# A decoder layer on one core: x tiles fetched at once and the first two projection tiles done per token tile, and a second query tile inside the residual loop

## The chip, the cores and the metric

The kernel runs on one core of a Trainium2 chip. The metric is the device time of one execution in microseconds. The engines are named as the profile names them: PE is TensorE (PEld its weight loads, which run beside the products), DVE is VectorE, ACT is ScalarE, POOL is GpSimd, SP is SyncE, which here only issues transfers.

## The reference, cut to what matters

One decoder layer for 512 prompt tokens and 64 sample tokens (8 sequences of 8), model width 2048, in float32:

```
h  = rmsnorm(x, g_mix_pre);  z = h @ w_in          # 56 column tiles of 128
mix = retention (8 heads) and differential attention (4 heads) over z
x  = x + rmsnorm(mix @ w_out, g_mix_post)
h  = rmsnorm(x, g_mem_pre);  q = h @ w_mem_q       # 4 query tiles of 128
x  = x + rmsnorm(softmax(q mk^T / sqrt(128)) mv @ w_mem_o, g_mem_post)
x  = x + rmsnorm(relu(rmsnorm(x, g_mlp_pre) @ w_up)**2 @ w_down, g_mlp_post)
mem_k, mem_v = rmsnorm(mem, mem_norm_g) @ w_mem_k, ... @ w_mem_v
```

Outputs are the new x, the new retention states, the new keys and values, and the memory keys and values.

## The kernel before, in words

**Layout.** Activations lie transposed: width on the 128 partitions (16 chunks), the 576 tokens along the free side. Every large product is made from two-part operands: a value is split into a high part (rounded, type fp32r) and a low part (the rest), for weights as `w_hi` and `w_lo`, for activations as `act_hi` and `act_lo`. One output tile of 128 columns by 576 tokens is the sum over 16 chunks of hi x hi, hi x lo and lo x hi, in two halves of 288 tokens that lie in two PSUM banks: 96 products. Each product carries its own weight load. The helper `parts` (line 1842) issues the six products of one chunk, `tile` (line 1850) a whole tile.

**Weights.** Stripes of 2048 columns of weights come by SP into `w_raw`, of which there are two. ACT copies a stripe to `w_hi` (helper `hi`, line 807), DVE subtracts to get `w_lo` (helper `lo`, line 1162). There are two buffers of each, so a stripe is split when the tile that used its buffer is through; semaphores `s_tile` (tiles done on PE), `s_evac` (tiles taken out of PSUM), `s_whi` and `s_wlo` (splits done) order this. All orders are written out by hand, one program for each engine.

**The opening** (lines 485 to 495 on SP, 624 to 638 on POOL, 815 to 859 on ACT, 1167 to 1225 on DVE, 1860 to 1928 on PE). x comes in seven tiles of 128 tokens, in the order prompt 0 to 3, sample (64 tokens), then two of memory. POOL asks for them, into two buffers `xin`: tile p waits till PE has turned tile p - 2 and ACT has squared it. The norm weights (seven of 16 rows, one of 2, and four lambda vectors) are gathered as 118 rows in `g_rows`: ACT issues eight loads, POOL four and the page table. When all of them and the page table are there (`s_gain`, `s_lam`), PE turns the rows into `gT` (line 1888). For each x tile PE turns it in four quarters (`x_turn`), DVE multiplies a quarter with the norm weights out of PSUM (steps g0 to g3), ACT rounds it to `act_hi`, and DVE subtracts for `act_lo` (steps l0 to l3). That is `x_norm`, on DVE in the order g0 g1 l0 g2 l1 g3 l2 l3. ACT squares each x tile as well; when all five are squared, a root, a reciprocal and five products with diagonals (line 1907) give `rstd_b`, the scale of each token, on all partitions. It is multiplied in when a tile is taken out of PSUM.

The first two projection tiles use `half_tile`: tokens 0 to 287 of tiles 0 and 1 when three x tiles are done, tokens 288 to 575 after the fifth. Then come x tile 5 and projection tile 2, x tile 6 and tile 3 (`early_tile`), the memory keys and values, and the main stream. Tiles 0 to 3 are rotated when they are taken out (`z_turn`, line 1240).

**The residual loop ahead of the query tiles** (ACT 1001, DVE 1618, PE 2210 and 2250 to 2255). For each of 16 chunks DVE scales y and adds it to x, ACT makes the high part and the square of it, DVE the low part (line 1615). PE sums the squares over the partitions with two products of ones of type f32 (each recorded as two, line 2218) and does the six products of the first query tile for that chunk (`first_tile`). Then ACT and DVE make the root and its reciprocal (1018, 1628), and three more query tiles follow, each with its own weight split, taken out with the scale at line 1657. `residual` and `first_tile` serve a second time ahead of the MLP.

Of the kernel before, what the change touches and what calls it, by code (L numbers as in the profile page):

```python
# [14 lines left out]
F32 = mybir.dt.float32  # L15
F32R = mybir.dt.float32r
I32 = mybir.dt.int32
ALU = mybir.AluOpType
# [142 lines left out]
def program(nc, x_prompt, x_sample, mem_prompt, state_ret, cache_k, cache_v, cache_mk, cache_mv, pages,  # L161
# [5 lines left out]
    with ctx:  # L167
# [48 lines left out]
        st = ExitStack()  # L216
        mem_hi = sb("mem_hi", [P, KC, MEM], F32R, st)
        mem_lo = sb("mem_lo", [P, KC, MEM], F32R, st)
        xin = [sb(f"xin{b}", [P, D], F32, st) for b in range(2)]
# [110 lines left out]

        c_wpad = z_out[0][:, 0:MC * C_PAD + 32]
# [12 lines left out]
        s_lam = sem("s_lam")  # L344
        s_rcs = sem("s_rcs")
# [10 lines left out]
        s_xin = [sem(f"s_xin{b}") for b in range(2)]  # L356
# [15 lines left out]
        EARLY = 4  # L372

# [245 lines left out]
        def _(pool):  # L619
# [16 lines left out]
            pool.dma_start(dcs[:], dcs_d).then_inc(s_dcs, 16)  # L636
            for p in range(2, len(order)):
                x_load(p)
# [37 lines left out]

            page = [pool.value_load(pg[0:1, i:i + 1], min_val=0, max_val=NPOOL - 1) for i in range(DB * NPG)]
# [124 lines left out]
        def _(act):  # L802
# [12 lines left out]
            for g, row in ((g_mix_pre, G_MIX_PRE), (g_mix_post, G_MIX_POST), (g_mem_pre, G_MEM_PRE), (g_mem_post, G_MEM_POST),  # L815
                           (g_mlp_pre, G_MLP_PRE), (g_mlp_post, G_MLP_POST), (g_memn, G_MEMN)):
                act.dma_start(g_rows[row:row + KC, :], g.rearrange("a (c p) -> (a c) p", p=P)).then_inc(s_gain, 16)
            act.dma_start(g_rows[G_SUB:G_SUB + 2, :], subln.rearrange("a (c p) -> (a c) p", p=P)).then_inc(s_gain, 16)

            def x_norm(p):  # L820

                t = order[p]
                rows = x_tiles[t][1]
                act.wait_ge(s_xin[p % 2], 16 * (p // 2 + 1))
                act.wait_ge(e_act.sem, e_act.before("sq", p))
                e_act.did(nc.scalar.activation(sq_junk[0:rows, :], xin[p % 2][0:rows, :], ACT.Square,
                                               accum_out=ssq[0:rows, t:t + 1]), "sq")
# [25 lines left out]
            x_norm(5)  # L853
            hi(4, 0, 0, 3)
            x_norm(6)
            act.wait_ge(e_act.sem, e_act.of("sq", NT + 1))
# [144 lines left out]
            def residual(k, g_pre, stripe, tile):  # L1001

                hi(stripe + 1, 0, (stripe + 1) % 2, tile + EXTRA)
                roots(2 * k)
                with act.Fori(0, KC // 2) as i:
                    for b in range(2):
                        act.wait_ge(n_x, i * 2 + (k * KC + b + 1))
                        act.sem_inc(s_idle, 1)
                        x = xT[:, bass.ds(2 * i + b, 1), :].rearrange("p a t -> p (a t)")
                        nc.scalar.activation(act_hi[:, bass.ds(2 * i + b, 1), :].rearrange("p a t -> p (a t)"), x,  # L1010
                                             ACT.Copy, scale=gT[:, bass.ds(2 * i + (g_pre + b), 1)]).then_inc(n_hi, 1)

# [28 lines left out]
            for j in range(1, MH):  # L1041
                hi(S_MQ + j + 1, 0, (j + 1) % 2, G_MQ + EXTRA + j)
# [111 lines left out]
        def _(dve):  # L1154
# [15 lines left out]
            for k in range(2):  # L1170
                V.tensor_tensor(lamv[:, k:k + 1], gT[:, G_LAM + 2 * k:G_LAM + 2 * k + 1], gT[:, G_LAM + 2 * k + 1:G_LAM + 2 * k + 2],
                                ALU.mult).then_inc(m_dve, 1)

            V.tensor_scalar(gT[:, G_SUB:G_SUB + 2], gT[:, G_SUB:G_SUB + 2], 1.0 - LAM_INIT, None, ALU.mult).then_inc(m_dve, 1)

# [23 lines left out]
            x_norm(0)  # L1199
            dve.wait_ge(m_act, 1)  # L1200
# [5 lines left out]
            x_norm(1)  # L1206
            lo(0, 0)
            x_norm(2)
            lo(1, 1)
# [30 lines left out]
            def z_turn(n, b, stored):  # L1240
# [7 lines left out]
                for half in range(2):  # L1248
                    cols = slice(half * TH, (half + 1) * TH)
                    ins = V.tensor_tensor(z_out[b][:, cols], G[2 * b + half][:, 0:TH], rstd_b[:, cols], ALU.mult)  # L1250
# [400 lines left out]
            for j in range(MH):  # L1651
                if j:
                    lo(S_MQ + j + 1, (j + 1) % 2)
                dve.wait_ge(s_tile, G_MQ + EXTRA + j + 1)
                for half in range(2):
                    cols = slice(half * TH, (half + 1) * TH)
                    ins = V.tensor_tensor(c_q[:, j, cols], G[2 * (j % 2) + half][:, 0:TH], rstd_b[:, cols], ALU.mult)
                ins.then_inc(s_evac, 1)

# [176 lines left out]
        def _(pe):  # L1836
# [23 lines left out]
            def x_turn(p):  # L1860
                rows = x_tiles[order[p]][1]
                pe.wait_ge(s_xin[p % 2], 16 * (p // 2 + 1))
                for q in range(4):
                    if p >= 1:
                        pe.wait_ge(e_dve.sem, e_dve.of(f"g{q}", p - 1))
                    for j in range(4):
                        ins = nc.tensor.transpose(A[q][:, j * P:j * P + rows], xin[p % 2][0:rows, (4 * q + j) * P:(4 * q + j + 1) * P],
# [15 lines left out]

            pe.wait_ge(s_cst, 16)
            x_turn(0)
            pe.wait_ge(s_gain, 16 * 8)
            pe.wait_ge(s_lam, 16 * 5)
            nc.tensor.transpose(G[0][:, 0:G_ROWS], g_rows[:], ident[0:G_ROWS, 0:G_ROWS]).then_inc(m_pe, 1)
# [3 lines left out]
            for p in range(1, 4):  # L1892
                x_turn(p)
            pe.wait_ge(s_wlo, 1)
            pe.wait_ge(e_dve.sem, e_dve.of("l3", 2))
            pe.wait_ge(m_act, 1)
            half_tile(0, 0)
            x_turn(4)
            pe.wait_ge(s_wlo, 2)
            half_tile(1, 0)  # L1900
            for c in range(NT):
                rows = tok(c)[1]
                pe.wait_ge(m_dve, 7 + c)
                if c == 0:
                    pe.wait_ge(e_dve.sem, e_dve.of("l3", NT - 1))
# [317 lines left out]

            def out_tile(n):
# [26 lines left out]
            first_tile(0, S_MQ, G_MQ)  # L2251
            for j in range(1, MH):
# [213 lines left out]
```

## Time and profile before

| what | us |
|---|---|
| median of 3 runs (3130.74 to 3131.6) | 3131.55 |
| the profiled execution | 3132.76 |
| its span, first to last instruction | 3131.1 |
| PE busy in it | 3042.4 |
| DVE busy | 1301.3 |
| ACT busy | 768.9 |

The profile is of one execution. Engine shares are of the span; a row of a group names line, engine, operation and tiles with count, busy time and mean duration. Ends of matmuls are modelled and they overlap, so the time from the start of one to the start of the next says more of PE's pace than a duration does.

### The profile page before, as it was taken

To read this page: it belongs to the slowest core of one execution; us is meant where nothing else is said; L and a number is where in the kernel's file an instruction comes from. 1 tells how busy PE (TensorE), PEld (TensorE's weight loads), DVE (VectorE), ACT (ScalarE), POOL (GpSimd) and SP (SyncE) were. 2 spreads that over 40 slices of the span, in tenths; PEclk is the share of its full clock that TensorE was granted. 3 is DMA by queue.
4 is the path that set the end of the run, shared out by engine and by line. 5 is a ranking of instruction groups with operands and counts; after the bars stand their busy time and mean duration, and the time that the engine had idled before them with its cause. 6 is when DMAs were issued, how large, how long until landed. Compare 5 with 4: busy or idle time off the path is not lost.

```text
span 3131.1 us, 53528 instructions
## 1 busy us (share of the span) xinstructions
PE 3042.4 (97%) x22485; PEld 2931.0 (94%) x22485; DVE 1301.3 (42%) x1860; ACT 768.9 (25%) x836; POOL 165.1 (5%) x265
## 2 busy tenths in 40 slices
PE   7999999999999998998999999999999999999996
PEld 6899999989899997787999999999999999999995
DVE  6544245445554536467332322323323233232346
ACT  4311123223222233334212112122121121221221
POOL 0000012221211010000000000000000000000001
PEclk9999999999999999999999999999999999999997
DMA  5433535554656361513222223222222222222241
GB/s 181 156 103 107 151 117 162 167 168 149 218 162 222 134 211 54 148 55 115 81 80 81 91 73 89 82 80 80 80 80 86 77 87 86 80 80 80 80 141 61
DMA packets 398904, 355.04 MB, mean 113 GB/s; under 512 B 9554, under 2 KB 362052, under 8 KB 396772
## 3 DMA queue, kind: packets, MB, share of 16 engines
q1 hardware_dynamic: 377456, 269.18, 28.7%
q0 software_dynamic: 21136, 84.66, 7.9%
q8 instruction: 56, 0.92, 0.1%
q14 instruction: 28, 0.23, 0.0%
q10 hardware_dynamic: 228, 0.06, 0.0%
HBM read 305.62 MB, written 48.23 MB: 113 GB/s over the span
## 4 chain that ended last, share of the span: by engine, by line
PE 90%; issue 4%; DVE 3%; DMA 1%; POOL 1%; ACT 1%; DVEq 0%; POOLq 0%; ACTq 0%
PE gemm L1846 81%; PE aux L1949 2%; PE gemm L1926 1%; PE gemm L1875 1%; DVE yT L1606 1%; DVE yT L1827 1%; PE aux L1989 1%; PE aux L2005 1%; DMA d_vp<-in_cache_diff_v 0%; POOL d_kp L682 0%; POOL d_vp L682 0%; ACT w_hi L812 0%; DVE rstd_b L1596 0%; DMA pg<-in_page_table 0%; PE aux L2152 0%
## 5 line engine op out<-in xcount | busy, mean ns | idle before, releaser
L1846 PE MATMUL gemm<-act_hi,w_hi 128*128 128x288 f32 x4544 | 994.8, 300 | 7.8 <-DVE act_lo L1615 4.3
L1846 PE MATMUL gemm<-act_hi,w_lo 128*128 128x288 f32 x4544 | 973.4, 296 | 0.0
L1846 PE MATMUL gemm<-act_lo,w_hi 128*128 128x288 f32 x4544 | 972.7, 296 | 0.0
L1846 PEld LDWEIGHTS gemm<-act_hi,w_hi 128*128 128x128 f32 x4544 | 731.6, 189 | 41.2 <-issue 18.1
L1846 PEld LDWEIGHTS gemm<-act_lo,w_hi 128*128 128x128 f32 x4544 | 732.6, 189 | 0.0
L1846 PEld LDWEIGHTS gemm<-act_hi,w_lo 128*128 128x128 f32 x4544 | 732.6, 189 | 0.0
L1165 DVE TENSOR_TENSOR w_lo<-w_raw,w_hi 128x2048 fp32r<-128x2048 f32 x216 | 494.4, 2289 | 198.3 <-ACT w_hi L812 74.2
L1846 PE MATMUL gemm<-u_lo,w_hi 128*128 128x288 f32 x2048 | 438.6, 296 | 0.0
L1846 PE MATMUL gemm<-u_hi,w_hi 128*128 128x288 f32 x2048 | 438.5, 296 | 0.0
L1846 PE MATMUL gemm<-u_hi,w_lo 128*128 128x288 f32 x2048 | 438.4, 296 | 0.0
L1846 PEld LDWEIGHTS gemm<-u_hi,w_hi 128*128 128x128 f32 x2048 | 330.2, 189 | 0.0
L1846 PEld LDWEIGHTS gemm<-u_lo,w_hi 128*128 128x128 f32 x2048 | 330.2, 189 | 0.0
L1846 PEld LDWEIGHTS gemm<-u_hi,w_lo 128*128 128x128 f32 x2048 | 330.2, 189 | 0.0
L812 ACT ACTIVATE w_hi<-w_raw 128x2048 fp32r<-128x2048 f32 x90 | 172.1, 1912 | 335.8 <-PE gemm L1846 280.0
L1118 ACT ACTIVATE w_hi<-w_raw 128x2048 fp32r<-128x2048 f32 x63 | 120.8, 1918 | 516.6 <-PE gemm L1846 516.6
L1777 DVE TENSOR_TENSOR yT<-yT,gemm 128x288 f32 x192 | 78.5, 450 | 362.9 <-PE gemm L1846 362.9
L1755 DVE SCALAR_TENSOR_TENSOR z_out<-gemm,rstd_b 128x288 f32<-128x288 f32 x128 | 52.6, 452 | 405.1 <-PE gemm L1846 405.0
L1110 ACT ACTIVATE z_out<-z_out 128x576 f32<-128x576 f32 x64 | 43.9, 685 | 613.8 <-DVE z_out L1755 613.8
L1105 ACT ACTIVATE w_hi<-w_raw 128x2048 fp32r<-128x2048 f32 x63 | 120.1, 1906 | 77.4 <-PE gemm L1846 76.1
L794 POOL DMA_DIRECT2D act_hi<-x_scratch x1 | 0.6, 574 | 1818.6 <-PE gemm L1846 1818.6
L1760 DVE TENSOR_TENSOR u_lo<-z_out,u_hi 128x576 f32 (+1 forms) x64 | 48.5, 758 | 112.4 <-ACT u_hi L1112 112.4
L1235 DVE TENSOR_TENSOR z_out<-gemm,rstd_b 128x288 f32<-128x288 f32 x48 | 19.7, 451 | 99.1 <-PE gemm L1846 99.1
(309 smaller groups left out, 1922.9 us busy)
## 6 DMA issues: line engine op xcount, KB each, us to landing
w_raw<-in_w_mlp_up SPq DMA_DIRECT2D x64, 1024.0 KB, 6.4
w_raw<-in_w_mlp_down SPq DMA_DIRECT2D x64, 1024.0 KB, 5.3
w_raw<-in_w_in SPq DMA_DIRECT2D x56, 1024.0 KB, 5.7
w_raw<-in_w_out SPq DMA_DIRECT2D x16, 1024.0 KB, 6.0
z_scratch<-z_out SPq DMA_DIRECT2D x56, 288.0 KB, 2.1
r_zin<-z_scratch POOLq DMA_DIRECT2D x8, 1152.0 KB, 6.3
xin<-in_x_prompt POOLq DMA_DIRECT2D x8, 1024.0 KB, 6.8
d_z<-z_scratch POOLq DMA_DIRECT2D x12, 576.0 KB, 7.1
```

The source lines that it names most:

```text
L812: nc.scalar.activation(w_hi[b][:], w_raw[b][:], ACT.Copy).then_inc(s_whi, 1)
L1105: nc.scalar.activation(w_hi[(b + 1) % 2][:], w_raw[(b + 1) % 2][:], ACT.Copy).then_inc(s_whi, 1)
L1110: nc.scalar.activation(u_s[:], u_t[:], ACT.Square).then_inc(u_sq, 1)
L1118: nc.scalar.activation(w_hi[(b + 1) % 2][:], w_raw[(b + 1) % 2][:], ACT.Copy).then_inc(s_whi, 1)
L1165: V.tensor_tensor(w_lo[b][:], w_raw[b][:], w_hi[b][:].bitcast(F32), ALU.subtract).then_inc(s_wlo, 1)
L1606: V.tensor_tensor(y, y, n_rt[:], ALU.mult).then_inc(n_t, 1)
L1755: ins = V.scalar_tensor_tensor(out=u_t[:, cols], in0=G[2 * b + half][:, 0:TH], scalar=0.0, in1=rstd_b[:, cols], op0=ALU.max, op1=ALU.mult)
L1760: V.tensor_tensor(u_lo[:, k, :].rearrange("p a t -> p (a t)"), u_s[:], u_hi[:, k, :].rearrange("p a t -> p (a t)").bitcast(F32), ALU.subtr ...
L1777: ins = V.tensor_tensor(y, y, G[2 * m + half][:, 0:TH], ALU.add)
L1827: V.scalar_tensor_tensor(out=yT[:, c, :], in0=yT[:, c, :], scalar=gT[:, G_MLP_POST + c:G_MLP_POST + c + 1], in1=x_back[:, c, :], op0=ALU.m ...
L1846: ins = M(out[half][:, 0:TH], w[b][:, cols], x[:, k, half * TH:(half + 1) * TH], start=first and n == 0, stop=last and n == 2)
L1949: return nc.tensor.transpose(out, in_, ident[0:rows, 0:rows])
```

## The change

**Opening.** There are five `xin` buffers, three of them in the room of `mem_hi` and `mem_lo`; POOL asks for all five x tiles at once and for the page table after them, and waits for that only where it reads it. The lambda rows and three of the gains are issued by SP, which waits for them ahead of the first weight stripe; ACT issues five loads. PE turns the norm weights first. ACT runs a Square of one column early, splits w0 behind x tile 0 and w1 behind x tile 1, and squares each x tile behind its rounding. DVE puts the split of w0 ahead of the lambda steps. `half_tile` is replaced by `piece(n, p)`: projection tile n for x tile p, 48 products of 128 tokens (64 for the sample), the prompt in one bank and the sample in the next. At the evacuation of tiles 0 and 1 the columns are cut at 512 and not at 288.

**Residual loop.** In the first use `first_tiles` does the second query tile four chunks behind the first, in two more banks. The third weight stripe is split behind the loop, ahead of root and reciprocal; the third query tile goes to banks of its own (`q_bank`) without a wait for an evacuation. The second use, ahead of the MLP, stays.

```diff
+        x_early = [sb(f"x_early{b}", [P, D], F32, alias) for b in range(PC - 1)]
-        xin = [sb(f"xin{b}", [P, D], F32, st) for b in range(2)]
+        xin = [sb(f"xin{b}", [P, D], F32, st) for b in range(2)] + x_early
+        q_bank = [G[0:2], G[2:4], A[0:2], G[2:4]]
...
             sp.dma_start(cst[:], cst_d).then_inc(s_cst, 16)
+            for k, v in enumerate((lq1, lk1, lq2, lk2)):
+                sp.dma_start(g_rows[G_LAM + k:G_LAM + k + 1, :], v).then_inc(s_lam, 16)
+            for g, row in gains[4:]:
+                sp.dma_start(g_rows[row:row + KC, :], g.rearrange("a (c p) -> (a c) p", p=P)).then_inc(s_lam, 16)
+            sp.wait_ge(s_lam, 16 * (4 + len(gains[4:])))
...
             def x_load(p):
                 src, rows = x_tiles[order[p]]
-                if p >= 2:
-                    pool.wait_ge(e_pe, 4 * (p - 1))
-                    pool.wait_ge(e_act.sem, e_act.of("sq", p - 2))
-                pool.dma_start(xin[p % 2][0:rows, :], src).then_inc(s_xin[p % 2], 16)
-
-            x_load(0)
-            x_load(1)
-            for k, v in enumerate((lq1, lk1, lq2, lk2)):
-                pool.dma_start(g_rows[G_LAM + k:G_LAM + k + 1, :], v).then_inc(s_lam, 16)
-            pool.dma_start(pg[:], pages.rearrange("(a b) n -> a (b n)", a=1)).then_inc(s_lam, 16)
+                if p >= NT:
+                    pool.wait_ge(e_pe, 4 * (p - NT + 1))
+                    pool.wait_ge(e_act.sem, e_act.of("sq", p - NT))
+                pool.dma_start(xin[p % NT][0:rows, :], src).then_inc(s_xin[p % NT], 16)
+
+            for p in range(NT):
+                x_load(p)
+            pool.dma_start(pg[:], pages.rearrange("(a b) n -> a (b n)", a=1)).then_inc(s_pg, 16)
...
             act.wait_ge(s_setup, 3)
+            nc.scalar.activation(rms[:, 0:1], eps[:], ACT.Square)
             x_norm(0)
+            hi(0, 0, 0, None)
+            x_square(0)
             act.wait_ge(m_pe, 2)
             nc.scalar.activation(lamv[:, 2:4], G[1][:, 0:2], ACT.Exp).then_inc(m_act, 1)
             x_norm(1)
-            hi(0, 0, 0, None)
+            hi(1, 0, 1, None)
+            x_square(1)
             x_norm(2)
-            hi(1, 0, 1, None)
             x_norm(3)
+            x_square(2)
             x_norm(4)
+            x_square(3)
+            x_square(4)
...
+                if k == 0:
+                    hi(stripe + 2, 0, stripe % 2, tile + EXTRA + 1)
                 for half in range(2):
                     act.wait_ge(n_used, (k + 1) * KC + 2)
...
             x_norm(0)
+            lo(0, 0)
+            for k in range(2):
+                V.tensor_tensor(lamv[:, k:k + 1], ...
+            x_norm(1)
+            lo(1, 1)
             dve.wait_ge(m_act, 1)
...
-            x_norm(1)
-            lo(0, 0)
             x_norm(2)
-            lo(1, 1)
...
                 low(k, KC - 1, g_pre)
+                if k == 0:
+                    lo(stripe + 2, stripe % 2)
                 dve.wait_ge(n_rts, 4 * k + 4)
...
-            def half_tile(n, half):
-
+            def piece(n, p):
+
+                c0, rows = tok(p)
+                out = G[2 * n][:, c0:c0 + rows] if p < PC else G[2 * n + 1][:, 0:rows]
+                pe.wait_ge(s_wlo, n + 1)
+                pe.wait_ge(e_dve.sem, e_dve.of("l3", p))
                 for k in range(KC):
                     for i, (w, x) in enumerate(((w_hi, act_hi), (w_hi, act_lo), (w_lo, act_hi))):
-                        ins = M(G[2 * n + half][:, 0:TH], w[n][:, k * P:(k + 1) * P], x[:, k, half * TH:(half + 1) * TH],
+                        ins = M(out, w[n][:, k * P:(k + 1) * P], x[:, k, c0:c0 + rows],
                                 start=k == 0 and i == 0, stop=k == KC - 1 and i == 2)
                 return ins
...
             pe.wait_ge(s_cst, 16)
+            pe.wait_ge(s_gain, 16 * 5)
+            pe.wait_ge(s_lam, 16 * (4 + len(gains[4:])))
+            nc.tensor.transpose(G[0][:, 0:G_ROWS], g_rows[:], ident[0:G_ROWS, 0:G_ROWS]).then_inc(m_pe, 1)
             x_turn(0)
...
+            x_turn(1)
             pe.wait_ge(m_dve, 4)
             pe.wait_ge(s_setup, 3)
             M(G[1][:, 0:2], ones[:], lamv[:, 0:2], start=True, stop=True).then_inc(m_pe, 1)
...
+            piece(0, 0)
+            x_turn(2)
+            piece(0, 1)
+            piece(1, 0)
+            x_turn(3)
+            piece(1, 1)
+            piece(0, 2)
+            x_turn(4)
+            piece(1, 2)
+            piece(0, 3)
+            piece(1, 3)
             pe.wait_ge(m_act, 1)
-            half_tile(0, 0)
-            x_turn(4)
-            pe.wait_ge(s_wlo, 2)
-            half_tile(1, 0)
+            piece(0, 4).then_inc(s_tile, 1)
             for c in range(NT):
...
                 M(out, ones[0:rows, :], diag_t[c % 2][0:rows, 0:rows], start=True, stop=True).then_inc(m_pe, 1)
-            for n in range(2):
-                half_tile(n, 1).then_inc(s_tile, 1)
+            piece(1, 4).then_inc(s_tile, 1)
...
+            def first_tiles(stripe, tile, behind):
+                pe.wait_ge(s_wlo, stripe + 2)
+                pe.wait_ge(s_evac, tile)
+                def chunk(m, c):
+                    return parts((stripe + m) % 2, c, slice(c * P, (c + 1) * P), act_hi, act_lo, G[2 * m:2 * m + 2], c == 0, c == KC - 1)
+                for c in range(KC):
+                    pe.wait_ge(n_xsq, c + 1)
+                    for half in range(2):
+                        ins = M(A[2 + half][:, 0:TH], ones[:], n_sq[c % 2][:, half * TH:(half + 1) * TH], start=c == 0, stop=c == KC - 1)
+                    ins.then_inc(n_used, 1)
+                    if c >= behind:
+                        chunk(1, c - behind)
+                    pe.wait_ge(n_lo, c + 1)
+                    ins = chunk(0, c)
+                ins.then_inc(s_tile, 1)
+                for c in range(KC - behind, KC):
+                    ins = chunk(1, c)
+                ins.then_inc(s_tile, 1)
...
-            first_tile(0, S_MQ, G_MQ)
-            for j in range(1, MH):
+            first_tiles(S_MQ, G_MQ, 4)
+            for j in range(2, MH):
                 pe.wait_ge(s_wlo, S_MQ + j + 1)
-                pe.wait_ge(s_evac, G_MQ + j - 1)
-                tile(j % 2, P, 0, KC, act_hi, act_lo, j % 2).then_inc(s_tile, 1)
+                if j == 3:
+                    pe.wait_ge(s_evac, G_MQ + j - 1)
+                for k in range(KC):
+                    ins = parts(j % 2, k, slice(k * P, (k + 1) * P), act_hi, act_lo, q_bank[j], k == 0, k == KC - 1)
+                ins.then_inc(s_tile, 1)
```

## Rows read from the trace of the kernel before

**Rows 1.** The page, busy time of each engine and the costliest group.
```profile
PE 3042.4 (97%) x22485; PEld 2931.0 (94%) x22485; DVE 1301.3 (42%) x1860; ACT 768.9 (25%) x836; POOL 165.1 (5%) x265
...
L1846 PE MATMUL gemm<-act_hi,w_hi 128*128 128x288 f32 x4544 | 994.8, 300 | 7.8 <-DVE act_lo L1615 4.3
```
**Rows 2.** Chain of waits, 0 to 145 us: start us, us, what.
```profile
4.68 10.02 DMA pg<-in_page_table
...
36.84 7.96 PE gemm L1875 x48
...
52.46 0.23 PE aux L1907 x2
...
54.32 13.00 PE gemm L1875 x96
67.32 1.75 PE aux L1867 x16
69.06 12.78 PE gemm L1846 x96
```
**Rows 3.** Timeline, 0 to 70 us: start us, us, engine, line, tiles.
```profile
10.18 3.65 PE L1867 MATMUL aux<-cst,xin 128*128 128x128 f32 x16 [10.18 <-DMA xin<-in_x_prompt]
...
15.83 1.41 DVE L1189 TENSOR_TENSOR gx<-aux,gT 128x512 f32<-128x512 f32 x2
...
20.19 1.43 DVE L1196 TENSOR_TENSOR act_lo<-gx,act_hi 128x512 fp32r<-128x512 f32 x2
...
39.38 0.44 PE L1875 MATMUL gemm<-act_lo,w_hi 128*128 128x288 f32 x1
...
39.62 0.44 PE L1875 MATMUL gemm<-act_hi,w_lo 128*128 128x288 f32 x1
...
39.85 0.34 PE L1875 MATMUL gemm<-act_hi,w_hi 128*128 128x288 f32 x1
...
61.12 0.82 DVE L1250 TENSOR_TENSOR z_out<-gemm,rstd_b 128x288 f32<-128x288 f32 x2 [5.94 <-PE gemm L1875]
...
65.20 2.27 DVE L1165 TENSOR_TENSOR w_lo<-w_raw,w_hi 128x2048 fp32r<-128x2048 f32 x1
```
**Rows 4.** Busy time by stretch: PE, PEld, DVE, ACT, POOL, then granted clock, DMA.
```profile
36.80:39.80 3.00, 2.96 (x12) 2.99 (x13) 2.02 (x1) 2.84 (x3) 0.00 (x0) 1.00 0.88 186
```
**Rows 5.** Chain of waits, 1205 to 1310 us.
```profile
1250.06 0.76 DVE yT L1606
...
1252.43 0.76 DVE yT L1606
...
1261.85 39.20 PE gemm L1846 x294
```
**Rows 6.** Timeline of PE in the residual loop, with a backlog.
```profile
1233.79 1.13 PE L2218 MATMUL aux<-z_out,ones 128*128 128x288 f32 x4
...
1235.56 1.13 PE L2218 MATMUL aux<-z_out,ones 128*128 128x288 f32 x4
```
**Rows 7.** DMA issues of the first 100 us: size, median us to landing.
```profile
w_raw<-in_w_in SPq DMA_DIRECT2D x4, 1024.0 KB, 11.2
...
cst<-const_cst SPq DMA_DIRECT2D x1, 194.0 KB, 2.7
...
```
**Rows 8.** Timeline of PE and PEld: spacing of long and of short products.
```profile
107.99 0.39 PE L1926 MATMUL gemm<-w_hi,mem_hi 128*128 128x512 f32 x1
108.22 0.39 PE L1926 MATMUL gemm<-w_hi,mem_lo 128*128 128x512 f32 x1
...
813.88 0.99 PEld L2160 LDWEIGHTS aux<-r_v,r_kd 128*128 128x128 f32 x8
...
832.09 1.20 PEld L2194 LDWEIGHTS aux<-ones,r_sq 128*128 128x128 f32 x10
```
**Rows 9.** Groups of PEld by shape: 128 and 32 weight columns.
```profile
L1926 PEld LDWEIGHTS gemm<-w_lo,mem_hi 128*128 128x128 f32 x64 | 12.0, 188 | 2.5
...
L2340 PEld LDWEIGHTS aux<-c_vc,z_out 128*32 128x32 f32 x128 | 3.2, 109 | 3.0 <-issue 3.0
```

More of the change, by code:

```diff
@@ L344, in program @@
         s_lam = sem("s_lam")
+        s_pg = sem("s_pg")
         s_rcs = sem("s_rcs")
@@ L355, in program @@
         s_evac = sem("s_evac")
-        s_xin = [sem(f"s_xin{b}") for b in range(2)]
+        s_xin = [sem(f"s_xin{b}") for b in range(NT)]
         s_zst = [sem(f"s_zst{b}") for b in range(2)]
@@ L372, in program @@
         EARLY = 4
+        gains = ((g_mix_pre, G_MIX_PRE), (g_mix_post, G_MIX_POST), (g_mem_pre, G_MEM_PRE), (g_mem_post, G_MEM_POST),
+                 (g_mlp_pre, G_MLP_PRE), (g_mlp_post, G_MLP_POST), (g_memn, G_MEMN))
         block = ctx.enter_context(nc.Block())
@@ L625, in x_load @@
                 src, rows = x_tiles[order[p]]
-                if p >= 2:
-                    pool.wait_ge(e_pe, 4 * (p - 1))
-                    pool.wait_ge(e_act.sem, e_act.of("sq", p - 2))
-                pool.dma_start(xin[p % 2][0:rows, :], src).then_inc(s_xin[p % 2], 16)
-            x_load(0)
-            x_load(1)
-            for k, v in enumerate((lq1, lk1, lq2, lk2)):
-                pool.dma_start(g_rows[G_LAM + k:G_LAM + k + 1, :], v).then_inc(s_lam, 16)
-            pool.dma_start(pg[:], pages.rearrange("(a b) n -> a (b n)", a=1)).then_inc(s_lam, 16)
+                if p >= NT:
[5 more added lines that the diff above has]
+            pool.dma_start(pg[:], pages.rearrange("(a b) n -> a (b n)", a=1)).then_inc(s_pg, 16)
             pool.dma_start(dcs[:], dcs_d).then_inc(s_dcs, 16)
-            for p in range(2, len(order)):
+            for p in range(NT, len(order)):
                 x_load(p)
@@ L812, in hi, with x_square @@
                 nc.scalar.activation(w_hi[b][:], w_raw[b][:], ACT.Copy).then_inc(s_whi, 1)
-            for g, row in ((g_mix_pre, G_MIX_PRE), (g_mix_post, G_MIX_POST), (g_mem_pre, G_MEM_PRE), (g_mem_post, G_MEM_POST),
-                           (g_mlp_pre, G_MLP_PRE), (g_mlp_post, G_MLP_POST), (g_memn, G_MEMN)):
+            for g, row in gains[0:4]:
                 act.dma_start(g_rows[row:row + KC, :], g.rearrange("a (c p) -> (a c) p", p=P)).then_inc(s_gain, 16)
             act.dma_start(g_rows[G_SUB:G_SUB + 2, :], subln.rearrange("a (c p) -> (a c) p", p=P)).then_inc(s_gain, 16)
+            def x_square(p):
+                t = order[p]
+                rows = x_tiles[t][1]
+                act.wait_ge(s_xin[p % NT], 16 * (p // NT + 1))
+                act.wait_ge(e_act.sem, e_act.before("sq", p))
+                e_act.did(nc.scalar.activation(sq_junk[0:rows, :], xin[p % NT][0:rows, :], ACT.Square,
+                                               accum_out=ssq[0:rows, t:t + 1]), "sq")
             def x_norm(p):
@@ L823, in x_norm @@
                 rows = x_tiles[t][1]
[L824 to L827, printed above, removed]
                 for q in range(4):
@@ L853, in _ @@
             x_norm(5)
+            x_square(5)
             hi(4, 0, 0, 3)
             x_norm(6)
+            x_square(6)
             act.wait_ge(e_act.sem, e_act.of("sq", NT + 1))
@@ L1169, in _ @@
             dve.wait_ge(m_dve, 1)
[L1170 to L1174, printed above, removed]
             def x_norm(p):
@@ L1199, in _ @@
             x_norm(0)
+            lo(0, 0)
+            for k in range(2):
+                V.tensor_tensor(lamv[:, k:k + 1], gT[:, G_LAM + 2 * k:G_LAM + 2 * k + 1], gT[:, G_LAM + 2 * k + 1:G_LAM + 2 * k + 2],
+                                ALU.mult).then_inc(m_dve, 1)
+            V.tensor_scalar(gT[:, G_SUB:G_SUB + 2], gT[:, G_SUB:G_SUB + 2], 1.0 - LAM_INIT, None, ALU.mult).then_inc(m_dve, 1)
+            x_norm(1)
+            lo(1, 1)
             dve.wait_ge(m_act, 1)
@@ L1247, in z_turn @@
                 dve.wait_ge(D_ROT.sem, D_ROT.before("z", n))
-                for half in range(2):
-                    cols = slice(half * TH, (half + 1) * TH)
-                    ins = V.tensor_tensor(z_out[b][:, cols], G[2 * b + half][:, 0:TH], rstd_b[:, cols], ALU.mult)
+                split = TP if early and n < 2 else TH
+                for half, cols in enumerate((slice(0, split), slice(split, T))):
+                    ins = V.tensor_tensor(z_out[b][:, cols], G[2 * b + half][:, 0:cols.stop - cols.start], rstd_b[:, cols], ALU.mult)
                 D_ROT.did(ins, "z")
@@ L1651, in _ @@
             for j in range(MH):
-                if j:
-                    lo(S_MQ + j + 1, (j + 1) % 2)
+                if j == MH - 1:
+                    lo(S_MQ + MH, MH % 2)
                 dve.wait_ge(s_tile, G_MQ + EXTRA + j + 1)
@@ L1656, in _ @@
                     cols = slice(half * TH, (half + 1) * TH)
-                    ins = V.tensor_tensor(c_q[:, j, cols], G[2 * (j % 2) + half][:, 0:TH], rstd_b[:, cols], ALU.mult)
+                    ins = V.tensor_tensor(c_q[:, j, cols], q_bank[j][half][:, 0:TH], rstd_b[:, cols], ALU.mult)
                 ins.then_inc(s_evac, 1)
+                if j == 1:
+                    lo(S_MQ + j + 2, j % 2)
             for c in range(MC):
@@ L1866, in x_turn @@
                     for j in range(4):
-                        ins = nc.tensor.transpose(A[q][:, j * P:j * P + rows], xin[p % 2][0:rows, (4 * q + j) * P:(4 * q + j + 1) * P],
+                        ins = nc.tensor.transpose(A[q][:, j * P:j * P + rows], xin[p % NT][0:rows, (4 * q + j) * P:(4 * q + j + 1) * P],
                                                   ident[0:rows, 0:rows])
                     ins.then_inc(e_pe, 1)
-            def half_tile(n, half):
+            def piece(n, p):
[3 more added lines that the diff above has]
+                pe.wait_ge(e_dve.sem, e_dve.of("l3", p))
                 for k in range(KC):
                     for i, (w, x) in enumerate(((w_hi, act_hi), (w_hi, act_lo), (w_lo, act_hi))):
-                        ins = M(G[2 * n + half][:, 0:TH], w[n][:, k * P:(k + 1) * P], x[:, k, half * TH:(half + 1) * TH],
+                        ins = M(out, w[n][:, k * P:(k + 1) * P], x[:, k, c0:c0 + rows],
                                 start=k == 0 and i == 0, stop=k == KC - 1 and i == 2)
@@ L2250, in _ @@
             sums()
-            first_tile(0, S_MQ, G_MQ)
-            for j in range(1, MH):
+            first_tiles(S_MQ, G_MQ, 4)
+            for j in range(2, MH):
                 pe.wait_ge(s_wlo, S_MQ + j + 1)
-                pe.wait_ge(s_evac, G_MQ + j - 1)
-                tile(j % 2, P, 0, KC, act_hi, act_lo, j % 2).then_inc(s_tile, 1)
+                if j == 3:
[3 more added lines that the diff above has]
+                ins.then_inc(s_tile, 1)
             pe.wait_ge(c_mkin, 16)
```

14 lines of the change are left out of this document (4 added, 10 removed).

## The prediction

> **What bounds the kernel now.** The page first: TensorE is busy for 97% of the span, nearly all of it in 288-column products of the projection helper [rows 1]. So time is to be won only where PE stands still, and whatever adds to PE's own work on the path costs its full length. Then the chain of waits of the first 145 us [rows 2]: nothing of the projection runs before 36.84 us; ahead of it lie a load that lands at 14.70 us (the page table, last of the set that the turning of the norm weights waits for), and then a chain of VectorE. Four half tiles of 48 products each follow, and tile 2 starts at 69.06 us. From there the order is the same in both kernels, so **the start of tile 2 is the mark for the opening**.
>
> The timeline shows what fills the time before 36.84 us [rows 3]: one token tile takes VectorE from 15.83 to 21.62 us (5.8 us, eight steps of 0.7), one weight split 2.27 us. It shows TensorE's clock too: the first products start every 0.23 us (288 columns at 1.2 GHz) until 39.85 us, while those of tile 2 start every 0.133 us (12.78/96), at 2.4 GHz [rows 2]; the turns of x before them, 16 in 3.65 us, are at the lower level as well. The granted clock reads 1.00 all through this stretch [rows 4], so here the spacing tells the level and the column does not. The slow products lasted for 3.0 us.
>
> Second place: the residual loop ahead of the query tiles. VectorE gives one chunk every 2.37 us (1250.06 to 1252.43) [rows 5], and where PE has a backlog it does a chunk in 1.77 us (1233.79 to 1235.56) [rows 6]. So 0.6 us of each chunk is free on PE. After the loop three whole tiles take 38.4 of the 39.20 us to 1301.05 [rows 5].
>
> **Part 1, loads and norm weights.** All five x tiles are asked for at once; the reload wait on PE and the squares goes for four of the five. Lambda rows and three gains move from POOL and ACT to SP, and SP now waits for them before it asks for the first weights. SP's eight small issues at the 0.44 us of such an issue end at about 5 us; a small load took 2.7 us when little else ran [rows 7]. The norm weights are thus all there at 6.9 us at the earliest, and at 14.7, as now, at the latest; I take 8, nearer to the small load, since these no longer stand behind two megabytes on POOL's queue. The price is that w0 is asked for at 8 instead of 1.3 us: it shares with the x tiles, and at half of some 360 GB/s (1.05 MB, 5.8 us, and about 2 us to begin) it lands at about 16. This queue's four loads took 11.2 us in the median [rows 7], which would be 19.
>
> Then: norm weights turned at 8, x tile 0 turned from 8.5, VectorE's first step at 9.3, last at about 15.2 (6.4 us ahead of 21.6). The split of w0: ACT 16.0 to 17.9, VectorE to 20.2, three lambda steps 0.4 us, the two tiny products 0.6. PE's first piece starts at **21 us** (bounds 20 and 28), against 36.84. That is 16 us won on the start. The early dummy Square and the squares put behind the copies are on ACT and hidden: VectorE, not ACT, is the longer chain per tile.
>
> **Part 2, pieces per token tile: the term that decides.** Before, tiles 0 and 1 are 4 x 48 = 192 products of 288 columns, every 0.133 us: 25.5 us. After, they are 10 x 48 = 480 products of 128 or 64 columns, and each product still brings its own weight load of 128 columns. No row shows a 128-column product of this type. A product of 512 columns starts every 0.23 us and one of 288 every 0.133 [rows 2, 8]: 0.43 ns a column and 9 ns each, so 128 columns alone would take 0.065 us. That is the lower bound. But the weight load is not shortened with the columns: 188 ns each for 128 weights, 109 for 32 [rows 9], so 0.82 ns a weight column, some 105 ns of streaming. Where products are short, the loads set the pace: eight loads in 0.99 us (0.80/7 = 0.114 us) beside 128-column products, and ten in 1.20 us (about 0.112) beside products of one column [rows 8]. The ten are what settles it, for their columns cost next to nothing. I take **0.114 us**; above, 0.126 if the two shorter loads of the ten are counted at half.
>
> The Trainium skill (TensorE: Matmul & The Clock Gate, LDWEIGHTS) gives a weight load of 128 columns 107 ns; the rows agree. The same page (Back-to-back issue gap) gives pairs of load and product at 128 columns 81 ns each in a real kernel; with that the pieces would take 39 us and the kernel would come out a little faster. Its section on fast weight load excepts FP32 weights, and no row here shows a load of such weights under that.
>
> PE's sum from 21 us: 3.0 us at the lower clock (14 products at 0.22), 466 by 0.114 = 53.1, two turns of x of 1.75 and one of 1.1 (half the columns), the broadcast 1.9 (52.46 to 54.32 now) [rows 2]. That is 62.6 us, end at 83.6. Over that time VectorE, whose whole chain is 5 tiles and 2 splits (some 32 us), is done with each tile before PE asks for it: the bound moves from VectorE to PE. Piece (0,4) ends at 83.6 - 5.5 - 1.9 = 76.2; then broadcast 1.9, copies of rstd 0.9, rotation of tile 0 4.1 (61.12 to 65.2) and the split of w2 2.3 [rows 3] give 85.4; the turn of x tile 5 ends at 85.4 too. Tile 2 starts at 85.5 instead of 69.06: **+16.4 us**.
>
> **Part 3, second query tile in the loop.** Chunks 4 to 15 get six more products, 0.80 us: 2.56 us a chunk, above the 2.37 of VectorE, so PE sets the pace. From 1235.56: 12 x 2.56 = 30.7, loop end 1266.3 (now 1262.65). Four late chunks 3.2: 1269.5. The third weight split waits for the first tile's end: ACT 1.9, VectorE 2.3, to 1270.5, 1.0 us of PE idle. Two tiles of 12.8: 1296.1 instead of 1301.05: **-4.9 us**. The root and its reciprocal slip behind that split, to about 1274.3; evacuations of tiles 0 and 1 follow by 1276 and the last split by 1278.3, beside tile 2 (to 1283.3), and the third tile has banks of its own. If the loop's extra products were not hidden at all the part would be worth 0; if all 12.8 us went, -12.8.
>
> **Sum.** +16.4 - 4.9 = +11.5 us. The profiled execution took 3132.8 us (span 3131.1), 1.2 above the median 3131.55; so 3144.3 by its own count and **3143** against the median. This kernel's runs can tell about 0.2% (6.3 us) from no change.
>
> **Rivals.**
> - *The pieces cost by columns* (0.065 us each). Then VectorE stays the bound: its last tile at 46, rstd at 55.6 as now, split of w2 at 62.0; tile 2 7.0 us earlier, with part 3 -11.9: 3120. This is the other side; it decides if the pitch is under 0.083, where 480 pieces just fill the time won. Against it speak the one-column products. Chance 0.06.
> - *Loads overlap in part, or the pieces start early* (pitch 0.081 to 0.107). At 0.081: PE ends at 68.2, tile 2 at 70.0, sum -4: 3128; at 0.107 3140. The page's 81 ns is this one. Chance 0.10.
> - *The clock stays at 1.2 GHz*: pieces stream 53 of every 114 ns, and the sixteen turns from 10.18 us did not raise it [rows 3]. 480 at 0.22 = 106 us, turns doubled: tile 2 at 140, sum +66: 3198. For: nothing so thin starts from the low clock in this trace. Against: the heads, full of short products, keep the high one. Chance 0.06.
> - *Short products are run as plain f32 ones are*, two recorded instructions each: 384 at 0.228 and 96 at 0.114, 44 us more: 3187. Nothing for it but that no row excludes it. Chance 0.06.
>
> **Numbers.** Forecast case 0.72: 3134 to 3156 (pitch 0.110 to 0.126, start 20 to 28, part 3 from -5 to 0), mostly 3138 to 3150. The range takes in the partial overlap: 3127 to 3156, which leaves out the first, third and fourth rival (0.18). Faster by over 0.2%: 0.08 (first rival and a bit of the second). Within: 0.16 (second rival, lowest part of the forecast). Slower: 0.76.
>
> **What would show it.** Right: first piece near 21 us; 48 weight loads of a piece in about 5.5 us, PEld busy near 100% and VectorE waiting for PE between tiles; tile 2 near 85; the loop's chunks 2.56 us apart and PE without idle in it; query tiles done 5 us earlier from the loop's start. Wrong: a pitch under 0.083, a first piece after 28, or a clock at half through the pieces.

## The result, and the profile after

The changed kernel takes **3163.01 us** (3161.14 to 3165.22, 4 runs) against 3131.14 (3130.71 to 3131.6, 4 runs) of the kernel before beside it: ratio 1.0102, interval [1.0085, 1.012]. It is slower, as forecast, but by 31.9 us and not by 11.5, outside the range. Its profiled execution took 3161.99 us (span 3160.3).

The page, the lines that answer to [rows 1]:
```profile
PE 3069.1 (97%) x22773; PEld 2967.5 (94%) x22773; DVE 1301.6 (41%) x1860; ACT 769.1 (24%) x837; POOL 163.4 (5%) x261
```
PE is busy 26.7 us more than before, with 288 products more (480 for 192). The loss lies in the opening. The chain of waits of the changed kernel (start us, us, what) answers to [rows 2]:
```profile
3.39 6.05 DMA g_rows<-in_mem_norm_g
9.46 13.78 DMA w_raw<-in_w_in
23.25 1.92 ACT w_hi L823
...
28.35 10.34 PE gemm L1907 x48
38.69 3.43 PE aux L1895 x16
42.12 11.33 PE gemm L1907 x96
...
55.23 10.67 PE gemm L1907 x96
...
67.04 22.20 PE gemm L1907 x192
89.24 2.81 PE aux L1942 x10
92.05 10.38 PE gemm L1907 x48
102.43 3.01 PE aux L1895 x16
105.44 12.79 PE gemm L1874 x96
```
Tile 2 starts at 105.44 us, before at 69.06 [rows 2]: +36.4 us, forecast +16.4. Three things are to be seen. The first piece starts at 28.35 and not at 21: it waits for a weight stripe that took 13.78 us to come. It takes 10.34 us, 0.215 us a product, where a later pair of pieces takes 10.67 for 96, 0.111 us. And the last piece, of only 64 columns a product, takes 10.38 us again. In the pieces between them that ran at the high clock the pace is close to the forecast (0.114).

The windows of the same profile (us; busy PE, PEld, DVE, ACT, POOL; granted clock; DMA share, GB/s) say what the two slow pieces have in common:
```profile
42.00:43.00 1.00, 1.00 (x7) 1.00 (x7) 0.97 (x2) 0.32 (x1) 0.00 (x0) 0.50 0.99 331
43.00:44.00 1.00, 1.00 (x9) 1.00 (x9) 0.97 (x2) 0.31 (x1) 0.00 (x0) 0.81 1.15 297
...
80.00:87.00 7.00, 7.00 (x66) 7.00 (x64) 0.00 (x0) 0.00 (x0) 0.00 (x0) 1.00 0.01 2
87.00:88.00 1.00, 1.00 (x11) 1.00 (x10) 0.00 (x0) 0.00 (x0) 0.00 (x0) 0.87 0.00 0
88.00:95.00 7.00, 7.00 (x31) 6.41 (x31) 3.48 (x10) 1.91 (x1) 0.00 (x0) 0.50 0.00 0
```
The granted clock is 0.50, that is 1.2 GHz, through the first piece and up to 43 us, and again from just before 88 to 104 us. The second fall comes while PE is without a gap in the first 64-column piece, which began at 83.10 us. The timeline of PE (start, us, engine, line, operation, tiles) shows the start-to-start time going from 0.11 to 0.21 us within it:
```profile
87.42 0.28 PE L1907 MATMUL gemm<-act_hi,w_hi 128*128 128x64 f32 x1
87.53 0.28 PE L1907 MATMUL gemm<-act_lo,w_hi 128*128 128x64 f32 x1
...
87.77 0.40 PE L1907 MATMUL gemm<-act_hi,w_hi 128*128 128x64 f32 x1
87.99 0.40 PE L1907 MATMUL gemm<-act_lo,w_hi 128*128 128x64 f32 x1
```
So PE looks 100% busy and runs at half its clock.

The residual loop, chain of waits, from where PE had caught up:
```profile
1271.56 1.59 PE gemm L1874 x12
1273.15 0.97 PE aux L2270 x4
1274.12 1.58 PE gemm L1874 x12
...
1301.26 1.93 ACT w_hi L823
1303.22 2.30 DVE w_lo L1190
1305.56 13.04 PE aux L1874 x96
1318.61 12.82 PE gemm L1874 x96
```
A chunk takes 2.55 us (forecast 2.56) with no gap on PE, and the last query tile ends at 1331.4, before at 1301.05 [rows 5]: +30.4. The opening had cost 36.4, so this part gives back 5 to 6 us (forecast 4.9).

### The profile page after: what moved, and what is told of

The parts are those of the page before. It is cut to its first block, busy times and chain, and to the rows that moved or that the text cites. A ratio compares the mean times of both kernels' runs of the same rounds, so it can differ in the third digit from the quotient of the medians.

```text
span 3160.3 us, 54107 instructions
## 1 busy us (share of the span) xinstructions
PE 3069.1 (97%) x22773; PEld 2967.5 (94%) x22773; DVE 1301.6 (41%) x1860; ACT 769.1 (24%) x837; POOL 163.4 (5%) x261
## 4 chain that ended last, share of the span: by engine, by line
PE 92%; DVE 3%; issue 3%; DMA 1%; ACT 1%; POOL 1%; DVEq 0%; SPq 0%; ACTq 0%; POOLq 0%
PE gemm L1874 81%; PE gemm L1907 2%; PE aux L1983 2%; PE gemm L1960 1%; DVE yT L1855 1%; PE aux L2023 1%; PE aux L2039 1%; PE aux L2270 1%; DMA w_raw<-in_w_in 0%; ACT w_hi L823 0%; PE aux L1874 0%; DVE yT L1630 0%; DMA d_vp<-in_cache_diff_v 0%; DVE rstd_b L1620 0%; PE aux L1895 0%
```

## The experiments

Three questions: does the cost lie in the opening alone; why did the first stripe come so late; and what does the lower clock cost, apart from the number of products? Each kernel was timed beside the kernel before on its chip; the median of the kernel before was 3131.0 to 3131.8 there, so a difference between two changed kernels that is taken from their medians can be off by some 0.7 us.

**1. The loop part alone**, on the kernel before: `first_tiles`, `q_bank` and the moved splits, nothing of the opening.

> The kernel before with only the change of the residual loop (second query tile four chunks behind, third split behind the loop). My theory, that the loop hides part of a tile and PE then sets its pace at 2.55 us a chunk: 5 us faster than before, about 3126. Rival, that the extra products push the root and the evacuations out and the gain is given back in cross-attention: within 1 us of before, 3131. The two traces so far give 35.6 us of shift ahead of the loop and 30.4 behind it.

3125.86 us (3124.52 to 3127.99, 10 runs) against 3131.44, ratio 0.9983 [0.9974, 0.9993]: **-5.6 us**. The part works as argued, and the opening of the changed kernel costs 31.9 + 5.6, some 37 us, which agrees with the 36.4 of the chain.

**2. Half tiles in place of pieces**, all else as changed.
```diff
-            piece(0, 0)
             x_turn(2)
-            piece(0, 1)
-            piece(1, 0)
             x_turn(3)
...
+            half_tile(0, 0)
             x_turn(4)
...
+            half_tile(1, 0)
...
-                split = TP if early and n < 2 else TH
+                split = TH
```


> The changed kernel with its new loads, its early weight splits and its loop, but tiles 0 and 1 in half tiles of 288 columns (192 products in place of 480). Theory P (the number of products, each at the price of its weight load, and the low clock that thin products bring, make the loss): tile 2 starts at about 75 us in place of 105.4, so 30 us off, 3133. Theory L (the late first weight stripe, which lands at 23.2 us, makes most of it): the start stays late and no more than 15 us come back, 3148 or more.

3137.20 us (3135.52 to 3138.87, 10 runs), ratio 1.0017 [1.0007, 1.0027]: 25.8 us less than the changed kernel, a little short of what was expected. The pieces are thus 26 of the 37 us. The other 11 (3137.2 - 3131.4 = 5.8, and the 5.6 that the loop part gives back) come with the new order of loads and splits even when the products are as before. Its chain of waits shows them:
```profile
9.55 12.45 DMA w_raw<-in_w_in
...
41.77 8.72 PE gemm L1903 x48
...
60.63 3.01 PE aux L1936 x10
63.64 14.53 PE gemm L1903 x96
```
The first product starts at 41.77, 4.9 us later than before [rows 2], though the norm weights are there at 9.5 us and not at 14.7: VectorE's program has the split of w0 right behind x tile 0, and stands waiting for the stripe for 7.0 us, with four x tiles behind it. A second wait is new: the squares, now behind the copies on ACT, end only at 58.2 us, then come the root and the broadcast (60.63). PE has run dry by then (it stands for 2.5 us), and the clock is at 0.52 in the window 60 to 65 (3.01 us for ten products that took 1.9 before). Tile 2 starts at 79.92, 10.9 us late.

**3. No 64-column products**: the sample piece is made 128 columns wide. It computes 64 columns of the last prompt tile a second time and leaves nothing out; where the tile is taken out of PSUM, these 64 are skipped.
```diff
+        SW = 128
...
-                out = G[2 * n][:, c0:c0 + rows] if p < PC else G[2 * n + 1][:, 0:rows]
+                w0 = SW if p == PC else rows
+                c0 += rows - w0
+                out = G[2 * n][:, c0:c0 + w0] if p < PC else G[2 * n + 1][:, 0:w0]
```


> The changed kernel with the sample piece of both tiles widened from 64 to 128 columns (the last 64 prompt tokens are computed a second time into columns that nobody reads). Theory C (the clock falls because 64 columns in every 111 ns are too thin a stream): the granted clock stays at full speed from about 43 to 106 us, and piece (0,4), the broadcast, piece (1,4) and the turn of x tile 5 take 5.3, 1.9, 5.3 and 1.75 us in place of 6.2, 2.8, 10.4 and 3.0: 8 us off, 3155. Rival (the fall has another cause, as the time since the rise or the wait for the roots): no change, 3163.

3153.95 us (3153.12 to 3154.79, 4 runs), ratio 1.0072 [1.0055, 1.0089]: 9.1 us less, by doing more. In its windows the clock is back at 1.00 from 42 us and stays there. Chain of waits:
```profile
28.46 10.34 PE gemm L1911 x48
...
89.92 5.51 PE gemm L1911 x48
95.42 1.77 PE aux L1897 x16
97.22 13.05 PE gemm L1876 x96
```
The last piece takes 5.51 us instead of 10.38: 0.115 us a product, the same as for half the columns at the high clock, so columns cost nothing here; the turn behind it takes 1.77 instead of 3.01. Tile 2 is 8.2 us earlier. Of that, 0.6 us was won ahead of the sample pieces, where the clock rose a little sooner than in the profile of the changed kernel, and 7.6 from there on.

**4. Dummy products before the pieces.** 46 products of ones by the identity, into a bank not yet used, fill PE's wait for w0; they only add work.
```diff
             x_turn(1)
+            pe.wait_ge(s_setup, 3)
+            for _ in range(46):
+                M(G[3][:, 0:P], ones[:], ident, start=True, stop=True)
             pe.wait_ge(m_dve, 4)
```


> The changed kernel with 46 products of ones and the identity (f32, 128 columns, into a bank that is not yet used) in PE's idle time between the second turn of x and the lambda product, about 16 to 26 us. Theory C (the low clock at 28 to 43 us is only the result of PE having stood still, and 128-column pieces hold the high clock once it is there): the first piece takes 5.3 in place of 10.3 us, the turn behind it 1.75 in place of 3.4, and 7 us come off, 3156. Rival (pieces of 128 columns that start at the high clock lose it, or the dummy products do not hold it): no change, 3163, or a little slower.

The executions do not agree. The profiled one took 3153.6 us, the three others 3164.68 to 3165.42. The median, 3164.89, has a ratio of 1.0107 [1.009, 1.0124]: no gain. The profiled one shows what a gain looks like, in its chain of waits:
```profile
27.25 5.42 PE gemm L1907 x48
...
83.73 10.38 PE gemm L1907 x48
94.11 2.98 PE aux L1895 x16
```
Its clock was 1.00 from the turns on, and the first piece took 5.42 us, not 10.34; the 64-column piece then fell to half all the same. Tile 2 starts at 97.09, 8.3 us earlier: 1.1 by an earlier start (the stripe landed at 22.3), 4.9 in the first piece, 1.7 in the turn (1.77 for 3.43), 0.7 in the next two pieces (10.67 for 11.33). The low clock at the start thus costs 7 us. By the times, one execution in four was spared it; in the three others the clock was not seen.

**5. Without SP's wait** for the small loads, so that w0 is asked for at 4.1 us and not at 9.5.
```diff
-            sp.wait_ge(s_lam, 16 * (4 + len(gains[4:])))
```


> The changed kernel without SP's wait for the small loads: the first two weight stripes are asked for at about 4 us in place of 9.5. Theory S (the two queues share the transfer engines evenly): w0 lands at about 14 to 16 us in place of 23.2, the first piece starts near 20 and 7 to 8 us come off, 3155. Rival Q (a stripe gets less than its half while x tiles are under way, so that asking earlier hardly helps; it also slows the x tiles): w0 after 20 us, 0 to 3 us off, 3160 or more.

3164.75 us (3161.88 to 3165.93, 4 runs), ratio 1.0103 [1.0087, 1.0118]: no change. Chain of waits:
```profile
4.10 19.20 DMA w_raw<-in_w_in
```
Asked for 5.4 us earlier, the stripe lands at the same time, 23.3 us. The wait that I had priced as the cost of moving the small loads cost nothing; something else holds the stripe.

**6. Dummies and wide sample piece together** (3 and 4).

> The changed kernel with both cures: the sample piece at 128 columns and the 46 products in the idle time ahead of the first piece. In its profiled execution the second alone took 9.4 us off, in its three timed ones nothing. Theory C (128 columns every 111 ns always hold the high clock once it is there, and the timed runs lost it in the 64-column pieces): all runs at 3144 to 3147. Rival H (whether pieces of 128 columns hold the clock differs from run to run): the runs fall into two groups, some near 3145 and some near 3155 or above, or the median stays at 3154.

3149.93 us (3148.42 to 3155.25, 4 runs), ratio 1.0056 [1.0041, 1.0072]. The profiled execution, 3155.25, was the slow one: its stripe landed at 24.5 us, the dummies were through 2.5 us before the first piece, the clock stood at 1.00 until about 29.9 us and then at 0.50 to about 43:
```profile
29.39 9.79 PE gemm L1911 x48
```
Three others at 3148.4 to 3150.5 are some 5 us faster. Whether they kept the clock is not shown, only their times. That 46 dummies were a fixed number and the landing of w0 was not (22.3 us in the profile of 4, 24.5 here) fits the scatter but was not tried by itself.

**7. Two spans.** What the first six teach, in one kernel: loop part kept, x tiles at once, no wait on SP, but tiles 0 and 1 in only two parts, tokens 0 to 255 (two x tiles) and 256 to 575, and the splits of w0 and w1 one x tile later, behind x tiles 1 and 2, so that VectorE does not stand waiting for it.
```diff
+            def span(n, part):
+                cols = slice(0, CUT) if part == 0 else slice(CUT, T)
...
+            span(0, 0)
             x_turn(3)
...
+            pe.wait_ge(s_wlo, 2)
+            span(1, 0)
             x_turn(4)
...
+            span(0, 1).then_inc(s_tile, 1)
```


> The loop part as changed; x tiles asked for at once; small loads on SP ahead of the weights, without the wait; the weight splits after the second and the third x tile; tiles 0 and 1 in two spans, tokens 0 to 255 after the second x tile and 256 to 575 after the fifth (192 products of 256 or 320 columns). Theory (with wide products VectorE's chain bounds the opening and now starts at 11 us in place of 15.8): tile 2 starts near 63.5 us, with the loop 11 us faster than before, 3120. Rival (the roots, which wait for squares and broadcast, or w0 hold it up as they did with the half tiles, where tile 2 started at 79.9): no better than the loop alone, 3126 or more.

**3124.43 us** (3122.68 to 3127.16, 11 runs), ratio 0.9978 [0.9969, 0.9987]: faster than both kernels, but 4 us short of what was expected. Chain of waits:
```profile
4.31 19.13 DMA w_raw<-in_w_in
...
27.76 8.31 PE gemm L1904 x48
...
47.85 9.83 PE gemm L1904 x48
...
59.55 7.23 PE gemm L1904 x48
...
68.52 12.79 PE gemm L1874 x96
```
Tile 2 starts only 0.5 us earlier than before, though the first product starts 9 us earlier. PE waits for VectorE's last x tile (44.0 to 47.9), and the first 320-column span then takes 9.83 us where the second takes 7.23: the clock was at 0.66 in the window 45 to 50 and 0.65 in 50 to 55. Nearly all of the gain is the loop part's; 1.4 us to experiment 1 is less than the intervals can tell apart.

**8 to 10. Weights ahead of the later x tiles.** POOL asks for x tiles 0 and 1 as before, for tile 2 when w0 has landed, for tiles 3 and 4 when w1 has. SP's wait is left out.
```diff
             for p in range(NT):
+                if p == 2:
+                    pool.wait_ge(s_wfull[0], 16)
+                if p == 3:
+                    pool.wait_ge(s_wfull[1], 16)
                 x_load(p)
```
8, on the changed kernel:

> The changed kernel without SP's wait, and with POOL asking for x tile 2 only when w0 is there and for x tiles 3 and 4 only when w1 is there (x tiles 0 and 1 at once, as in the kernel before). Theory Q (w0 landed at 23.2 us because the five x tiles took the DMA engines ahead of it, and that put the first piece at 28.4 instead of 21): w0 now stands behind two megabytes and its own one, lands at 12 to 14 us, the split of w0 is through at about 19.5, the first piece starts at 20 to 21, and tile 2 starts some 7 us earlier: about 3156 to 3158. Rival (w0 is late for a reason of its own, SP's queue or the address pattern of the stripe): first piece still at 28, 3163 to 3165. If x tile 2 comes too late by this (VectorE wants it at about 23 us), the first pieces start early but VectorE then waits for x: 3160.

9, the same with the wide sample piece:

> The same with the sample pieces 128 columns wide (64 columns recomputed). If the two causes (late w0, clock lost in the 64-column pieces) add up: 3163 - 7 - 9 = about 3147. What then stays against the kernel before is the stretch at the lower clock at the start of the pieces and the 0.111 us for each of 480 products, about +21 for the opening, -5 for the loop. If the low clock at the start is as long as before (15 us) or longer because the pieces start from a colder engine: 3147 to 3153; if the engine keeps the clock from the turns (idle gap now under 5 us): 3140.

10, the same order of loads in the two spans:

> The two-span version (tokens 0 to 255 and 256 to 575 for tiles 0 and 1, loop part kept) with the same order of loads. In it VectorE stood 2.3 us waiting for w0's high part before its first split. With w0 there at 13 that wait goes: first span at 25.3 instead of 27.8, each later tile of VectorE 2.3 us earlier, tile 2 at about 66.2 instead of 68.5: 3122, against 3124.4 for the two spans and 3125.9 for the loop part alone. If x tile 2 or 3 is now late on VectorE, no gain: 3124 to 3127.

Beside 3131.75 (14 runs): 8 took 3157.40 us (3155.88 to 3158.06, 5 runs), ratio 1.0081 [1.0067, 1.0095]; 9 took 3147.38 (3145.49 to 3149.36, 5 runs), 1.005 [1.0037, 1.0064]; 10 took 3124.78 (3123.47 to 3127.05, 10 runs), 0.9977 [0.9968, 0.9987]. In the timeline of POOL of 8 (start, us, engine, line, tiles, idle before and its releaser) one reads when the stripes landed:
```profile
14.33 0.53 POOL L640 DMA_DIRECT2D x_early<-in_x_prompt  x1 [11.57 <-DMA w_raw<-in_w_in]
17.85 0.53 POOL L640 DMA_DIRECT2D x_early<-in_x_prompt  x1 [2.99 <-DMA w_raw<-in_w_in]
```
w0 landed just before 14.33 us instead of at 23.3: **the three later x tiles, asked for at once, had held it back**. The chain of 8:
```profile
21.43 10.34 PE gemm L1910 x48
...
85.12 10.38 PE gemm L1910 x48
...
98.99 13.62 PE gemm L1877 x96
```
The first piece starts at 21.43, where the prediction had it, and tile 2 is 6.5 us earlier than in the changed kernel. Experiment 5 differs from this one by POOL's order alone; there tile 2 started at 105.95, 7.0 us later. The first piece is as slow as before, at clock 0.50 to about 36 us. In 9 the last piece costs 5.51 us and tile 2 starts at 90.81:
```profile
21.68 10.34 PE gemm L1914 x48
...
90.81 13.05 PE gemm L1879 x96
```
The two causes add: of the 31.9 us over the kernel before, the loads take off 6.2 (25.7 are left in 8) and the wide sample piece 10.0 more. What is left, 15.6 us, is 480 products in place of 192 and the low clock at the start, less the loop part. In 10 the load did come early, but the median did not move (3124.78 beside 3124.43): tile 2 starts at 67.34, 1.2 us earlier, and VectorE's chain of five x tiles and two splits, which ends at 46.5 and 47.8 us, sets the pace. Where little waits for the stripe, its landing is worth little.

## Why the prediction was wrong

Right: the direction; that PE's own work would become the bound of the opening; **0.114 us a product**, measured 0.111 (10.67/96), set by the weight loads and not by columns (0.115 for 128 columns in 3, and 64 columns no cheaper); the loop part, -5.6 for -4.9, by the steps given (2.56 us a chunk, measured 2.55; a split at the end that PE waits for, 1.2 us where 1.0 was forecast: it takes 4.3, and the four late chunks run beside most of it); norm weights there at 9.4 us, taken at 8.

Wrong, with the extra in tile 2's start, 20.0 us (36.4 for 16.4):

- **"It shares with the x tiles ... it lands at about 16."** It landed at 23.24, and the first piece started 7.3 us later than the 21 forecast, just past the bound of 28 that the sum had kept open. The queues did not share evenly: asked for at 9.5 or at 4.1 us (5), behind five x tiles, the stripe came at 23.3; behind two (8) it was there by 14.3. I had priced the wait on SP and not the three x tiles that POOL now asks for ahead of it: the moved step's DMAs were counted as bytes and not as a queue that goes first. Undone, it gave 6.5 us at tile 2 and 6.2 in the time (25.7 us over the kernel before in place of 31.9). It also makes VectorE, whose order puts the split of w0 ahead of x tile 1, stand for 7.0 us in experiment 2.
- **"3.0 us at the lower clock."** That was the length seen before with 288-column products. With 128-column pieces the low clock lasted from 28.35 to 43.4 us here and from 21.43 to 36 in 8, and 13 to 15 us in each of the six profiles whose first piece ran at it. Wider products left it sooner: after 5.2 us with 256 columns (7), after 4.8 and 3.0 with 288 (2, and the kernel before). The sum took a length from wide products and used it for thin ones. In none of the six did the first piece raise the clock in its some 10 us; it rose in the sixteen turns behind the piece or in the products right after them (here turns from 38.69 to 42.12 and the rise at 43.4; in 5 turns from 38.75, rise at 41.1), and the low stretch of the 64-column pieces ended in turns too (from 102.43, rise at 104.8). Whether the pieces alone would ever have raised it was not tried. It cost 3.4 us in the first piece (10.34 for the 6.9 forecast), 1.7 in the turn and 0.4 in the next pair: 5.5 us.
- **The clock rival was half right, and was put down as all or nothing.** I gave 0.06 to a clock that stays at 1.2 GHz for all 480 products and set tile 2 at 140 for it. What happened is a fall in the 64-column pieces alone: 4.9 us in piece (1,4), 0.9 in the broadcast, 1.3 in the turn behind it, and 0.3 where it began. That is 7.4 us by the terms of the sum; experiment 3 gave back 7.6 from the sample pieces on, 8.2 at tile 2 in all, and 9.1 in the median. At the high clock products of 64 columns do cost what those of 128 cost, as the sum had it, but they lose that clock.

7.3 + 5.5 + 7.4 is 20.2, and the products at the high clock were 0.003 us quicker than forecast; 20.0 were to be explained.

Not settled: why one execution of experiment 4 kept the high clock through the first pieces and others did not, what a wait for x or for the stripe must not exceed for it, and whether it was the turns that ended the low stretches. The granted clock of the timed executions was not seen by stretch.

The Trainium skill (DMA: Bandwidth & Descriptors, Queues, rings and completion order) says that each DMA engine goes round its queues packet by packet. Read as equal shares of the bytes, as the forecast did, the stripe asked for at 4.1 us would have come before the last x tiles, and the runs decide against that. Read as turns, the rule may still hold: a row of an x tile is 8 KB and a row of the stripe 512 B, so a turn need not carry the same bytes. Rows of other lengths were not tried.

## What to carry to other kernels

PE can read 100% busy while its clock is at half: look at the granted clock by stretch before a busy share is believed, and where weight loads set the pitch, try padding a thin product rather than leave it thin (here 64 columns made 128, 9.1 us less). When loads are brought forward, ask who comes behind them; here a stripe on one queue landed after everything that the other queue had just been given. A split of work into finer parts is worth only what the next engine in the chain can use: two parts, with the splits one x tile later, beat five by 40 us with the same loads (7 beside 5).

## What had not been expected of the hardware

- The order of landing. In the changed kernel the five x tiles (4.7 MB, POOL's queue), asked for from 1.5 to 3.8 us, took 6.3 to 15.7 us from issue to landing, so that the last was in by 19.5, and the stripe of 1 MB on SP's queue came behind them, whichever of two times it was asked for. It is no strict order: in the kernel before, with the stripe asked for first, at 1.3 us, x tiles 0 and 1 took 8.5 and 11.1 us, against 6.3 and 8.0 after, and the stripe 13.3.
- Products of 128 columns every 0.111 us hold the high clock for almost 40 us (44 to 83 us), with turns between them, and 64-column products at the same pitch, from 83.10 us on, lose it at about 87.7, within their first piece.
- Turns of x can raise the clock. In the changed kernel, timeline of PE:
```profile
9.80 4.87 PE L1895 MATMUL aux<-cst,xin 128*128 128x128 f32 x28
```
28 turns took 4.87 us, 0.174 each, where eight at the start take 1.72 in experiment 8 (0.215 each; its chain of waits has `10.37 1.72 PE aux L1898 x8`): the later ones ran at the high level, which then was lost while PE waited for w0. The Trainium skill (TensorE: Matmul & The Clock Gate, Part 4: PE-mode transpose) says that turns do not bring the high clock; here the spacing says they did, in this profile: 28 at 0.215 would have taken 6.0 us.
- The granted-clock column reads 1.00 from the span's start while that same spacing is 0.215 us. It can be trusted only behind the first change that it shows; ahead of it the spacing tells the level.
